# Two-layer hybrid decoder step on one core: in the prompt's attention, three PSUM banks for the turned probabilities and one for the results, in place of two and two

## The chip, the cores and the metric

One core of a Trainium2 chip runs the whole program. The metric is the device time of one execution in microseconds (us); of several runs the median counts. Engines are named as in the profile: PE (TensorE, matrix products; its weight loads are PEld), DVE (VectorE), ACT (ScalarE), POOL (GpSimd), SP (SyncE, which here only issues transfers). PSUM, into which PE writes, has 8 banks of 128 partitions by 512 fp32 values.

## The reference, cut to what matters

The program is one inference step of a two-layer decoder over 1024 prompt tokens and 32 new tokens. Layer 0 has sparse attention: an indexer has already chosen which keys each query may see, and the choice is an additive mask. The change concerns the prompt's attention alone:

```
s = einsum('nqgrd,nqkgd->nqgrk', q, k) * HEAD_DIM ** -0.5     # 8 heads, 2 key-value heads, HEAD_DIM 128
s = where(valid, s, -inf)
p = softmax(s, axis=-1)
o = einsum('nqgrk,nqkgd->nqgrd', p, v)                        # then o @ w_o, residual, MLP, layer 1, ...
```

## The kernel before

The program is a row of blocks, each with one stream of instructions for every engine, written by hand and tied by semaphores. Within a stream the order is as written: an instruction that waits holds back everything behind it on its engine. The block that changes is the prompt's attention, L1787 to L1917. The blocks before it leave the queries in `qt`, keys in `kt`, values in `vr`, the indexer's scores in `score`; the block after it multiplies the results, which lie in `qt`, by `w_o`.

The prompt's 1024 rows are 8 tiles of 128 rows (t = 0 to 7), and each tile has 8 heads, so `qk_list` has 64 entries, called steps n = 0 to 63 here, with t = n // 8. Step n needs keys of t + 1 tiles only. Each step runs through all engines:

- PE, `qk(n)`, L1809: products of queries and keys into one of two pairs of banks (banks 2 and 3, or 4 and 5). It waits until DVE has read the products of step n - 2.
- DVE, L1909 to L1912: adds the mask, takes the row's maximum, and negates it.
- ACT, L1865: the exponential, with the row's sum. DVE, L1883: the reciprocal of that sum (it stands in DVE's loop behind the maximum of the step after). POOL, L1876: the scaling.
- PE, `turn(n)`, L1820: turns the probabilities, tile by tile of 128 by 128, into a bank of their own, up to four tiles to a bank; so a step has one such filling for t up to 3 and two from t = 4 on. ACT, L1856: copies each filling into `pt`.
- PE, `pv(m, part)`, L1832: the products of probabilities and values. They are made for four heads at once (m = 0 to 15, two for each tile), in one bank, and a group's t + 1 products are spread over four parts, one to each iteration of PE's loop. DVE, `take_pv(m)`, L1888: copies the bank's 512 columns into `qt`.

PE's loop runs qk(n), turn(n - 3), then one part of `pv`: the part of n is `divmod(n - 7, 4)`. DVE's loop runs, for n: in tiles t = 2 to 6 from the second head on one of seven passes that make the next tile's mask (`mask_steps`, L1617 to L1633), then the maximum of step n, then the reciprocal of step n - 1, and in every fourth iteration one `take_pv`: `take_pv(m)` stands in iteration n = 11 + 4 m. In that same iteration PE's `pv(m + 1, 0)` stands, behind qk(n) and turn(n - 3). ACT's loop runs the exponential of n and then the copies of step n - 3.

The banks before: 0 and 1 by turns for results, 2 to 5 for the scores, 6 and 7 by turns for turned probabilities. The waits that go with them, in PE's stream:

```
if m >= 2: pe.wait_ge(p_copied, m - 1)     # turn: the filling two back has been copied by ACT
if m >= 2: pe.wait_ge(pv_empty, m - 1)     # pv, part 0: the result two back has been copied by DVE
```

For t = 0 to 2 part 0 of a group has no product (it holds products 0 to (t + 1) // 4 - 1), but its waits stand there all the same. Its other wait, for the copies of the group's last head, is in both kernels.

Of the kernel before, what the change touches and what calls it, by code (L numbers as in the profile page):

```python
# [24 lines left out]
GROUP = HEADS // KV  # L25
# [7 lines left out]
P = 128  # L33
# [110 lines left out]
def hybrid_step(nc, x_prompt, x_sample, cache_k, cache_v, cache_kidx, state_pool, page_table, c_prompt, c_sample,  # L144
# [3 lines left out]
    with ctx:  # L148
# [43 lines left out]
        vr = sb("vr", [P, TILES + 1, KW])  # L192
# [109 lines left out]
        pt = [put("pt0", [P, TILES, GROUP * P]), at("pt1", [P, TILES, GROUP * P], F32, whi.manual_sbuf_range[0])]  # L302
# [4 lines left out]
        def bank(i):  # L307
            return pair[i // 2][:, i % 2, :]
# [17 lines left out]
        def sem(name):  # L326
            return ctx.enter_context(nc.semaphore(name))
# [43 lines left out]
        p_t, p_copied, pv_ready, pv_empty = sem("p_t"), sem("p_copied"), sem("pv_ready"), sem("pv_empty")  # L371
# [111 lines left out]
        def raw8(slot):  # L483
            return wraw[:, slot, :].rearrange("p (k c) -> p k c", k=KT8)
# [1299 lines left out]

        qk_list = [(t, h) for t in range(TILES) for h in range(HEADS)]  # L1787
        turn_list = [(t, h, a) for t, h in qk_list for a in range((t + 4) // 4)]
        PV_AFTER = AHEAD + GROUP
        with nc.Block() as block:  # L1790
            @block.sync
            def _(sp):
                for u in range(U_O, U_O + 2):
                    load_unit(sp, u, raw8(u % 2), dsa_w_o[0, :, (u - U_O) * P:(u - U_O + 1) * P].rearrange(
                        "(k p) c -> p k c", p=P))

            def turns_of(n):
                return [(m, a) for m, (t, h, a) in enumerate(turn_list) if (t, h) == qk_list[n]]

            @block.tensor  # L1800
            def _(pe):
                def qk(n):
                    t, h = qk_list[n]
                    if n >= 2:
                        pe.wait_ge(neg_done, n - 1)
                    L = P * (t + 1)
                    for s in range((L + 511) // 512):
                        w = min(512, L - 512 * s)
                        ins = pe.matmul(pair[1 + n % 2][:, s, 0:w], qt[:, h, t * P:(t + 1) * P],  # L1809
                                        kt[:, h // GROUP, 512 * s:512 * s + w], start=True, stop=True)  # L1810
                    ins.then_inc(qk_ready, 1)

                def turn(n):
                    t, h = qk_list[n]
                    pe.wait_ge(prob_done, n + 1)
                    for m, a in turns_of(n):
                        if m >= 2:
                            pe.wait_ge(p_copied, m - 1)
                        for j in range(4 * a, min(4 * a + 4, t + 1)):
                            ins = pe.transpose(bank(6 + m % 2)[:, (j - 4 * a) * P:(j - 4 * a + 1) * P],  # L1820
                                               ss[:, n % SR, j * P:(j + 1) * P], ident)
                        ins.then_inc(p_t, 1)

                def pv(m, part):

                    t, g = divmod(m, KV)
                    if part == 0:
                        pe.wait_ge(p_copied, turns_of(GROUP * m + GROUP - 1)[-1][0] + 1)
                        if m >= 2:
                            pe.wait_ge(pv_empty, m - 1)  # L1830
                    for j in range(part * (t + 1) // GROUP, (part + 1) * (t + 1) // GROUP):
                        ins = pe.matmul(bank(m % 2), vr[:, j, g * P:(g + 1) * P], pt[m % 2][:, j, :], start=(j == 0),  # L1832
                                        stop=(j == t))
                    if part == GROUP - 1:
                        ins.then_inc(pv_ready, 1)

                N = len(qk_list)
                for n in range(N + PV_AFTER):
                    if n < N:
                        qk(n)  # L1840
                    if 0 <= n - AHEAD < N:
                        turn(n - AHEAD)
                    if n >= PV_AFTER:
                        pv(*divmod(n - PV_AFTER, GROUP))

            @block.scalar
            def _(act):
                def copies(n):
                    t, h = qk_list[n]
                    for m, a in turns_of(n):  # L1850
                        act.wait_ge(p_t, m + 1)
                        k = min(4, t + 1 - 4 * a)
                        q = 2 * t + h // GROUP
                        if h % GROUP == 0 and q >= 2:
                            act.wait_ge(pv_ready, q - 1)
                        act.activation(pt[q % 2][:, 4 * a:4 * a + k, (h % GROUP) * P:(h % GROUP + 1) * P],  # L1856
                                       bank(6 + m % 2)[:, 0:k * P].rearrange("p (j c) -> p j c", j=k),
                                       ACT.Copy).then_inc(p_copied, 1)

                N = len(qk_list)  # L1860
                for n in range(N + AHEAD):
                    if n < N:
                        L = P * (qk_list[n][0] + 1)
                        act.wait_ge(neg_done, n + 1)
                        act.activation(ss[:, n % SR, 0:L], ss[:, n % SR, 0:L], ACT.Exp,  # L1865
                                       bias=small[:, 4 + n % SR:5 + n % SR],
                                       scale=SC_ATT, accum_out=small[:, 8 + n % SR:9 + n % SR]).then_inc(exp_done, 1)
                    if n >= AHEAD:
                        copies(n - AHEAD)

            @block.gpsimd
            def _(pool):
                for n, (t, h) in enumerate(qk_list):
                    L = P * (t + 1)
                    pool.wait_ge(rec_done, n + 1)
                    pool.tensor_scalar(ss[:, n % SR, 0:L], ss[:, n % SR, 0:L], small[:, 12 + n % SR:13 + n % SR], None,  # L1876
                                       ALU.mult).then_inc(prob_done, 1)

            @block.vector
            def _(dve):  # L1880
                def recip(n):
                    dve.wait_ge(exp_done, n + 1)
                    dve.reciprocal(small[:, 12 + n % SR:13 + n % SR], small[:, 8 + n % SR:9 + n % SR]).then_inc(rec_done, 1)  # L1883

                def take_pv(m):
                    t, g = divmod(m, KV)
                    dve.wait_ge(pv_ready, m + 1)
                    dve.tensor_copy(qt[:, GROUP * g:GROUP * (g + 1), t * P:(t + 1) * P],  # L1888
                                    bank(m % 2).rearrange("p (r c) -> p r c", r=GROUP)).then_inc(pv_empty, 1)


                chain(dve, dve.memset(causal[:, 0:P], 0.0), "v", vchain)
                chain(dve, dve.tensor_copy(causal[:, P:2 * P], cst[:, C_CM:C_CM + P]), "v", vchain)
                N = len(qk_list)
                for n in range(N + PV_AFTER + 1):
                    if n < N:
                        t, h = qk_list[n]
                        L = P * (t + 1)
                        mask = score_of(t) if t in IDX_TILES else causal[:, P - t * P:2 * P]
                        if t + 1 in IDX_TILES[1:]:  # L1900

                            if h == 0:
                                masking = mask_steps(dve, COL_OF[t + 1])
                            else:
                                next(masking)
                        dve.wait_ge(qk_ready, n + 1)
                        if n >= SR:
                            dve.wait_ge(p_t, turns_of(n - SR)[-1][0] + 1)
                        chain(dve, dve.tensor_tensor_reduce(ss[:, n % SR, 0:L], wide(1 + n % 2)[:, 0:L], mask, 1.0,  # L1909
                                                            LEAST, ALU.add, ALU.max, small[:, n % SR:n % SR + 1]),  # L1910
                              "v", vchain)
                        dve.tensor_scalar(small[:, 4 + n % SR:5 + n % SR], small[:, n % SR:n % SR + 1], -SC_ATT, None,  # L1912
                                          ALU.mult).then_inc(neg_done, 1)
                    if 1 <= n <= N:
                        recip(n - 1)
                    if n >= PV_AFTER + GROUP and (n - PV_AFTER) % GROUP == 0:
                        take_pv((n - PV_AFTER) // GROUP - 1)  # L1917
# [623 lines left out]
```

## Time and profile before

| | |
|---|---|
| time, median of 3 runs | 2372.76 us (2372.74 to 2382.14) |
| the profiled execution | 2369.18 us, of which 2367.5 us are the span from first to last instruction |
| busy in the span | PE 2232.2 us (94%), DVE 1001.8 (42%), ACT 782.0 (33%), POOL 634.6 (27%) |
| the block of the change | from 489.7 us (first of L1809) to 661.6 us (last products of L1832) |

Times in the rows are us from the span's start. A row of the timeline has start, duration, engine, line, operation, output and inputs, shapes and count, and in brackets how long the engine stood idle before it and what released it. Ends of matmuls are modelled, and neighbours overlap by about 0.16 us in the rows: the 592 ns of a 128x512 product are spaced by 430 ns when PE runs on. An fp32 product shows as two records, a turned tile as one.

### The profile page before, as it was taken

How to read it: one execution, taken by the hardware profiler on the slowest of the kernel's cores; microseconds unless marked ns; L12 is line 12 of the kernel's file. 1: busy time of each engine (PE TensorE's matmuls, PEld its weight loads, DVE VectorE, ACT ScalarE, POOL GpSimd, SP SyncE). 2: the span in 40 equal slices, each digit the busy share in tenths (PEclk: the TensorE clock that was granted, in tenths of full speed). 3: DMA queues.
4: the chain of work that ended last, by engine and by line, in shares of the span. 5: the costliest groups of instructions: out<-in, count | busy, mean ns of one | idle time of the engine just before them, and what ended most of it. 6: DMA issues, size and time to landing. Idle time of an engine off the chain costs nothing. (4 is left out here: it accounts for less than half of the span.)

```text
span 2367.5 us, 37205 instructions
## 1 busy us (share of the span) xinstructions
PE 2232.2 (94%) x13836; PEld 2056.8 (87%) x13836; DVE 1001.8 (42%) x2431; ACT 782.0 (33%) x1414; POOL 634.6 (27%) x387
## 2 busy tenths in 40 slices
PE   5998899589989999999999999888999999999998
PEld 4885489245578999999999999888999999999998
DVE  2525788776435433233233332357333333323323
ACT  4204577655533312212212212354122122122124
POOL 4110111257736222222222222432222222222224
PEclk8998999889999999999999999899999999999999
DMA  8454464400032111111111112001111111111112
GB/s 301 140 171 128 148 207 156 144 18 1 0 127 80 54 45 50 49 44 44 44 44 51 46 44 65 27 19 45 46 45 45 44 46 52 45 44 44 44 44 82
DMA packets 208668, 170.29 MB, mean 72 GB/s; under 512 B 14477, under 2 KB 202109, under 8 KB 208565
## 3 DMA queue, kind: packets, MB, share of 16 engines
q1 hardware_dynamic: 201917, 154.64, 21.0%
q10 hardware_dynamic: 4160, 8.65, 1.0%
q0 software_dynamic: 2496, 5.77, 0.9%
q8 instruction: 55, 0.90, 0.2%
q14 instruction: 40, 0.33, 0.0%
HBM read 155.85 MB, written 11.64 MB: 71 GB/s over the span
## 5 line engine op out<-in xcount | busy, mean ns | idle before, releaser
L524 PE MATMUL pair<-hhi,whi 128*128 128x352 f32 x2184 | 716.6, 328 | 33.9 <-DVE hlo L725 8.8
L525 PE MATMUL pair<-hlo,whi 128*128 128x352 f32 x2184 | 705.0, 323 | 0.0
L526 PE MATMUL pair<-hhi,wlo 128*128 128x352 f32 x2184 | 704.6, 323 | 0.0
L2143 POOL TENSOR_TENSOR wlo<-wraw,whi 128x1024 fp32r<-128x1024 f32 x127 | 304.6, 2399 | 1145.1 <-ACT whi L2088 1143.9
L524 PE MATMUL pair<-hidh,whi 128*128 128x352 f32 x1536 | 495.4, 323 | 0.0
L525 PE MATMUL pair<-hidl,whi 128*128 128x352 f32 x1536 | 492.7, 321 | 0.0
L526 PE MATMUL pair<-hidh,wlo 128*128 128x352 f32 x1536 | 492.2, 320 | 0.0
L536 DVE SCALAR_TENSOR_TENSOR x<-pair,mod,x 128x352 f32<-128x352 f32 (+1 forms) x432 | 247.4, 573 | 514.6 <-PE pair L526 513.6
L524 PEld LDWEIGHTS pair<-hhi,whi 128*128 128x128 f32 x2184 | 412.3, 189 | 45.3 <-issue 25.0
L525 PEld LDWEIGHTS pair<-hlo,whi 128*128 128x128 f32 x2184 | 413.5, 189 | 0.4
L526 PEld LDWEIGHTS pair<-hhi,wlo 128*128 128x128 f32 x2184 | 412.3, 189 | 0.5
L2088 ACT ACTIVATE whi<-wraw 128x1024 fp32r<-128x1024 f32 x126 | 132.7, 1054 | 609.6 <-PE pair L526 609.6
L2195 DVE TENSOR_TENSOR squ<-relu 128x352 f32<-128x352 f32 x192 | 101.3, 527 | 492.0 <-ACT relu L2096 491.9
L525 PEld LDWEIGHTS pair<-hidl,whi 128*128 128x128 f32 x1536 | 288.5, 188 | 0.0
L524 PEld LDWEIGHTS pair<-hidh,whi 128*128 128x128 f32 x1536 | 288.3, 188 | 0.0
L526 PEld LDWEIGHTS pair<-hidh,wlo 128*128 128x128 f32 x1536 | 287.9, 187 | 0.0
L2096 ACT ACTIVATE relu<-pair 128x352 f32<-128x352 f32 x192 | 89.2, 464 | 471.1 <-PE pair L526 471.1
L494 POOL TENSOR_TENSOR wlo<-wraw,whi 128x1024 fp32r<-128x1024 f32 x36 | 89.1, 2476 | 282.0 <-ACT whi L490 281.9
L1876 POOL TENSOR_SCALAR ss<-ss,small 128x128 f32<-128x128 f32 (+7 forms) x64 | 118.5, 1856 | 79.9 <-DVE small L1883 79.5
L2199 DVE TENSOR_TENSOR hidl<-squ,hidh 128x352 fp32r<-128x352 f32 x192 | 105.0, 547 | 21.1 <-DVE squ L2195 1.9
L1452 ACT ACTIVATE junk_a<-score,cand 128x1024 f32<-128x1024 f32 (+2 forms) x93 | 84.0, 903 | 42.6 <-DVE cand L1533 31.2
L2098 ACT ACTIVATE hidh<-relu 128x352 fp32r<-128x352 f32 x192 | 95.9, 499 | 6.1
(282 smaller groups left out, 1955.3 us busy)
## 6 DMA issues: line engine op xcount, KB each, us to landing
wraw<-in_w_up_dram SPq DMA_DIRECT2D x64, 512.0 KB, 3.9
wraw<-in_w_down_dram SPq DMA_DIRECT2D x64, 512.0 KB, 3.4
mraw_i<-in_w_mod_dram SPq DMA_DIRECT2D x20, 1024.0 KB, 6.8
mraw_q<-in_w_mod_dram SPq DMA_DIRECT2D x12, 1024.0 KB, 5.1
mraw<-in_w_mod_dram SPq DMA_DIRECT2D x8, 1024.0 KB, 9.2
wraw<-in_dsa_w_in_dram SPq DMA_DIRECT2D x16, 512.0 KB, 6.0
mraw_w<-in_w_mod_dram SPq DMA_DIRECT2D x8, 1024.0 KB, 5.2
wraw<-in_dsa_w_o_dram SPq DMA_DIRECT2D x16, 512.0 KB, 4.1
```

The source lines that it names most:

```text
L494: pool.tensor_tensor(wlo[:, slot, :], wraw[:, slot, :], whi[:, slot, :], ALU.subtract).then_inc(lo_ready, 1)
L524: pe.matmul(out, a, hi[:, kr, r], start=(n == 0), stop=False)
L525: pe.matmul(out, a, lo[:, kr, r], start=False, stop=False)
L526: last = pe.matmul(out, b, hi[:, kr, r], start=False, stop=(n == len(ks) - 1))
L536: ins = dve.scalar_tensor_tensor(out=xs, in0=ps[:, 0:n], scalar=mod[:, layer, gate + d, 0:1], in1=xs, op0=ALU.mult, op1=ALU.add)
L1876: pool.tensor_scalar(ss[:, n % SR, 0:L], ss[:, n % SR, 0:L], small[:, 12 + n % SR:13 + n % SR], None, ALU.mult).then_inc(prob_done, 1)
L2088: act.activation(whi[:, slot(k), :], wraw[:, slot(k), :], ACT.Copy).then_inc(hi_ready, 1)
L2096: act.activation(relu[:, p % 3, :], up_bank(f, c, first)[:, 0:CW], ACT.Relu).then_inc(up_empty, 1)
L2098: act.activation(hidh[:, f, c * CW:(c + 1) * CW], relu[:, p % 3, :], ACT.Square).then_inc(square_done, 1)
L2143: pool.tensor_tensor(wlo[:, slot(k), :], wraw[:, slot(k), :], whi[:, slot(k), :], ALU.subtract).then_inc(lo_ready, 1)
L2195: dve.tensor_tensor(squ[:, p % 3, :], relu[:, p % 3, :], relu[:, p % 3, :], ALU.mult).then_inc(hid_square, 1)
L2199: dve.tensor_tensor(hidl[:, f, c * CW:(c + 1) * CW], squ[:, p % 3, :], hidh[:, f, c * CW:(c + 1) * CW], ALU.subtract).then_inc(hid_ready, 1)
```

## The change

The turned probabilities go through three banks by turns, 6, 7 and 1, and PE waits for the copy of the filling three back. All results go into bank 0, and part 0 of a group waits until DVE has copied the group just before. The copies of ACT and DVE read the banks so chosen. Nothing else differs.

```diff
+        T_BANK = (6, 7, 1)
 ...
                     for m, a in turns_of(n):
-                        if m >= 2:
-                            pe.wait_ge(p_copied, m - 1)
+                        if m >= 3:
+                            pe.wait_ge(p_copied, m - 2)
                         for j in range(4 * a, min(4 * a + 4, t + 1)):
-                            ins = pe.transpose(bank(6 + m % 2)[:, (j - 4 * a) * P:(j - 4 * a + 1) * P],
+                            ins = pe.transpose(bank(T_BANK[m % 3])[:, (j - 4 * a) * P:(j - 4 * a + 1) * P],
                                                ss[:, n % SR, j * P:(j + 1) * P], ident)
 ...
                     if part == 0:
                         pe.wait_ge(p_copied, turns_of(GROUP * m + GROUP - 1)[-1][0] + 1)
-                        if m >= 2:
-                            pe.wait_ge(pv_empty, m - 1)
+                        if m >= 1:
+                            pe.wait_ge(pv_empty, m)
                     for j in range(part * (t + 1) // GROUP, (part + 1) * (t + 1) // GROUP):
-                        ins = pe.matmul(bank(m % 2), vr[:, j, g * P:(g + 1) * P], pt[m % 2][:, j, :], start=(j == 0),
+                        ins = pe.matmul(bank(0), vr[:, j, g * P:(g + 1) * P], pt[m % 2][:, j, :], start=(j == 0),
                                         stop=(j == t))
 ...
                         act.activation(pt[q % 2][:, 4 * a:4 * a + k, (h % GROUP) * P:(h % GROUP + 1) * P],
-                                       bank(6 + m % 2)[:, 0:k * P].rearrange("p (j c) -> p j c", j=k),
+                                       bank(T_BANK[m % 3])[:, 0:k * P].rearrange("p (j c) -> p j c", j=k),
                                        ACT.Copy).then_inc(p_copied, 1)
 ...
                     dve.tensor_copy(qt[:, GROUP * g:GROUP * (g + 1), t * P:(t + 1) * P],
-                                    bank(m % 2).rearrange("p (r c) -> p r c", r=GROUP)).then_inc(pv_empty, 1)
+                                    bank(0).rearrange("p (r c) -> p r c", r=GROUP)).then_inc(pv_empty, 1)
```

## Rows read from the trace of the kernel before

**Rows 1.** Busy time by stretch (its us, busy by engine, granted clock, transfers).

```profile
core 0: us, PE busy (x) PEld busy (x) DVE busy (x) ACT busy (x) POOL busy (x), PEclk, DMA share, GB/s
489.00:497.00 8.00, 6.71 (x25) 5.19 (x26) 4.90 (x38) 4.63 (x21) 4.24 (x7) 0.57 0.48 134
497.00:520.00 23.00, 20.74 (x84) 11.59 (x83) 18.79 (x81) 14.66 (x48) 17.67 (x16) 1.00 0.00 1
...
583.00:612.00 29.00, 28.26 (x109) 15.45 (x108) 19.16 (x40) 15.15 (x32) 21.73 (x8) 1.00 0.00 1
612.00:645.00 33.00, 33.00 (x124) 17.68 (x123) 13.28 (x39) 17.31 (x33) 22.14 (x9) 1.00 0.00 0
...
662.00:670.00 8.00, 2.25 (x8) 2.28 (x9) 5.07 (x7) 6.26 (x14) 3.45 (x2) 0.62 0.78 286
```

**Rows 2.** Waits of PE in the block: who for whom, us, times, longest.

```profile
PE pair L1820 <- ACT pt L1856: 4.5, 10, 1.1
PE pair L1820 <- POOL ss L1876: 2.6, 5, 0.9
```

**Rows 3.** Timeline around iteration 59 (tile 7).

```profile
626.91 1.23 DVE L1909 CUSTOM_DVE_ANT_0 ss<-pair,score 128x1024 f32<-128x1024 f32 x1 [2.71 <-PE pair L1809]
627.59 1.02 PE L1832 MATMUL pair<-pt,vr 128*128 128x512 f32 x2
...
628.32 0.67 DVE L1888 COPY qt<-pair 128x512 f32<-128x512 f32 x1
```

**Rows 4.** Timeline: PE released by DVE in iteration 13.

```profile
500.71 0.15 DVE L1912 TENSOR_SCALAR small<-small 128x1 f32<-128x1 f32 x1
...
500.92 0.70 PE L1809 MATMUL pair<-kt,qt 128*128 128x256 f32 x2
```

**Rows 5.** Timeline around iteration 11 (tile 1).

```profile
500.26 0.60 PE L1809 MATMUL pair<-kt,qt 128*128 128x256 f32 x2
...
500.86 0.67 DVE L1888 COPY qt<-pair 128x512 f32<-128x512 f32 x1
```

**Rows 6.** Timeline around iterations 27 to 29 (tile 3).

```profile
525.46 1.11 PE L1809 MATMUL pair<-kt,qt 128*128 128x512 f32 x2
...
526.19 0.67 DVE L1888 COPY qt<-pair 128x512 f32<-128x512 f32 x1
...
526.84 1.56 DVE L1626 TENSOR_TENSOR_SCAN tie_run<-tie 128x640 f32<-128x640 f32 x1
...
528.43 0.69 DVE L1909 CUSTOM_DVE_ANT_0 ss<-pair,score 128x512 f32<-128x512 f32 x1
```

**Rows 7.** Timeline around iteration 31 (tile 3).

```profile
534.31 1.02 PE L1832 MATMUL pair<-pt,vr 128*128 128x512 f32 x2
...
535.04 0.67 DVE L1888 COPY qt<-pair 128x512 f32<-128x512 f32 x1
```

**Rows 8.** Timeline of iterations 43 to 45 (tile 5).

```profile
568.11 1.02 PE L1832 MATMUL pair<-pt,vr 128*128 128x512 f32 x2
...
568.89 0.67 DVE L1888 COPY qt<-pair 128x512 f32<-128x512 f32 x1
...
570.59 0.85 PE L1820 MATMUL pair<-cst,ss 128*128 128x128 f32 x6 [0.17 <-ACT pt L1856]
...
571.88 0.96 DVE L1909 CUSTOM_DVE_ANT_0 ss<-pair,score 128x768 f32<-128x768 f32 x1
...
574.72 0.84 PE L1820 MATMUL pair<-cst,ss 128*128 128x128 f32 x6 [1.13 <-ACT pt L1856]
```

**Rows 9.** Timeline of the block's end.

```profile
646.72 1.06 PE L1820 MATMUL pair<-cst,ss 128*128 128x128 f32 x8 [0.77 <-ACT pt L1856]
...
654.52 2.74 PE L1832 MATMUL pair<-pt,vr 128*128 128x512 f32 x6
654.72 0.69 DVE L1888 COPY qt<-pair 128x512 f32<-128x512 f32 x1 [8.44 <-PE pair L1832]
654.95 0.19 PEld L1832 LDWEIGHTS pair<-pt,vr 128*128 128x128 f32 x1 [0.24 <-issue]
```

## Prediction

> **What bounds the kernel now.** I first read the busy time by stretch. Over the block's last full tile, from 612 to 645 us, PE is busy for 33.00 of 33 us and nobody else for more than 22.14; in tile 6 it is 28.26 of 29; from tile 1 to the middle of tile 2 it is 20.74 of 23, with DVE at 18.79 [rows 1]. So PE sets the pace in the late tiles, and PE and DVE take turns in the early ones. The granted clock is 1.00, the level of 2.4 GHz, from 497 us on. The waits of PE come next: in the whole block it waited 4.5 us, in 10 places, for ACT's copies of turned probabilities, and 2.6 us for POOL [rows 2]. No row names a wait of PE for `pv_empty`: with two result banks that copy was always in time. Last I read the timeline at the places where the copy of a result and the next group's first products meet, iterations 11, 15, ... 67, fifteen in all.
>
> **What the change removes.** A third bank lets a filling start one copy earlier. All that it can give is what rows 2 show: 4.5 us. As the modelled ends overlap their successors by some 0.16 us, each of the 10 waits is really longer by that: 6.1 us at most, and nothing at least. Instructions, shapes and transfers stay as they were. The copies of ACT and DVE read other banks at the same price as long as nobody else touches those banks, and the semaphores see to that.
>
> **What it adds: a wait behind DVE's copy, fifteen times.** Take iteration 59. PE runs qk(59), turn(56), and then wants `pv(13, 0)`, whose first product starts at 627.59. With one bank it must wait for `take_pv(12)`. DVE issues that copy in the same iteration, behind the maximum of step 59 (1.23 us from 626.91), and this maximum had itself waited 2.71 us for qk(59). So the copy runs from 628.32 to 629.00 (0.67 us) [rows 3], 1.41 us after PE wants its bank. The copy is not slow; it is queued behind work that PE itself has only just released. Nothing makes DVE earlier when PE is later.
>
> To the difference comes the release. In iteration 13 PE started 0.06 us after DVE's negation had ended (500.86 to 500.92) [rows 4]. Then a weight load, 0.19 us [rows 9], must be made that normally lies under the product before. So 0.06 us if none of it shows, 0.25 if all; I take 0.15. One stall is then the copy's end, less the start that PE would have had, plus 0.15 us: 1.56 us in iteration 59.
>
> Behind the waiting part stand, on PE, the group's products, qk(n + 1) and turn(n - 2); DVE's next maximum waits for that qk, ACT's exponential for DVE, POOL for both. All move together, so a stall costs its whole length, unless PE would soon have waited for somebody who is not late.
>
> **The sum, in three parts.**
>
> *Iterations 11 to 27, five stalls* whose part 0 has no product; what waits is qk(n + 1). In the first, qk(12) starts at 500.26 and the copy ends at 501.53 [rows 5]; as PE next waited for POOL anyway, I count 0.8 us of it. In the last, qk(28) starts at 525.46 and the copy ends at 526.86 [rows 6]: about 1.5. The three between give about 1.1, 0.9 and 1.5 in the same reading, together some 5.8. In those of iterations 19 and 27 DVE goes straight from the copy into the scan of the mask pass (1.56 us from 526.84), and the next maximum, at 528.43, waits for the scan and not for qk(28), which even with the stall ends near 527.9. So I let most of these two, 1.6 us, be swallowed: **4.2 us** remain.
>
> *Iterations 31 to 55, seven stalls* with products. The first is 534.31 against a copy that ends at 535.71, 1.56 us with the release [rows 7]; that of iteration 43 is 568.11 against 569.56, 1.60 [rows 8]; the one of iteration 39, 1.5, is shorter in the rows only because PE had waited for ACT before it, and the other four lie between 1.5 and 1.65. Together 11.05 us. Here the third bank gives back. After iteration 43, PE waited 0.17 us and then 1.13 us for ACT's copies [rows 8], which came late because DVE's scan had pushed the maximum to 571.88. Now PE comes later by 1.6 us, DVE and ACT do not, and the first filling needs no fresh copy, so 1.6 us of it are gone again by iteration 45. In the same way I count back 1.45 in iterations 36 and 37, 0.35 each in 39 and 41, 0.2 in 50 and 0.85 in 52 and 53: 4.8 us in all, and **6.25 us** remain.
>
> *Iterations 59, 63 and 67.* Tile 7 has no mask pass, and PE does not wait. The stalls are 1.56, 1.55 and, in the drain, where the copy (654.72 to 655.41) no longer stands behind a maximum and the product would start at 654.52, 1.04 [rows 9]. Before turn(61) PE waited 0.77 us for ACT [rows 9], 0.93 without the overlap, and that is regained. **3.2 us** remain.
>
> The sum is 4.2 + 6.25 + 3.2 = 13.65 us: 21.0 us of stalls less 7.35 given back. The block's end moves by that, and with it the rest of the program: the next block's first work reads the last results, and its transfers are issued behind them. The profiled execution would go from 2369.18 to 2382.8 us, its span from 2367.5 to 2381.2. The median of the runs lies 3.6 us above the profiled execution; I put the same difference on it: 2372.76 + 13.65 = 2386.4 us, 0.58% slower.
>
> One rule of the Trainium skill speaks directly against the change. "Perfetto Trace Analysis", in the section on optimizing tensor performance, says that independent matmul groups should rotate through different PSUM banks, so that the evacuation of one overlaps the next group's matmuls. Priced as that sentence reads, one evacuation laid bare per group, it would be 15 times the copy's 0.67 us and the release, some 12 us before anything is given back. Rows 3 make it twice as dear, because the copy stands behind a maximum in DVE's queue.
>
> **The rivals.**
>
> *Nothing is given back.* If every wait for DVE, ACT and POOL moves along with PE, all 21.0 us stay: 2393.8 us. The rows of iterations 43 to 45 speak against it, since there DVE runs on its own work [rows 8]; for it speaks that in most iterations DVE had waited for qk. Chance 0.1.
>
> *The stalls of tiles 1 to 6 are swallowed* (the other side: not slower by what can be measured). Place: the mask pass of each tile, where DVE leads. If the two stalls of each tile, some 3.1 us, fit into the time by which PE is ahead of DVE and ACT there, only tile 7's 3.2 us remain: 2376.0 us. It decides from about 1.9 us given back by chance beyond my count, since 11.8 us is the bound below. For it: tile 5 swallows its first stall whole. Against it: in tile 6 PE stands idle for only 0.74 of 29 us [rows 1]. Chance of this and what lies between it and the bound: 0.22.
>
> *Only the gain.* If DVE's copy were in time, for a reason that I do not see in rows 3, the 6.1 us at most would be left: 2366.7 us, 0.26% faster and still no measurable change. Chance 0.03. The change can hardly be faster by more than 0.5%.
>
> *The clock falls.* The stalls thin PE's work most in tile 1. The granted clock was 0.57 and 0.62 in the stretches on both sides of the block, where PE stood still between products or for 6 us [rows 1]. If one stretch like that at the block's head, some 7 us, came back at 1.2 GHz, half of it, 3.4 us, would be added: 2389.8 us. Against it: it stayed at 1.00 through waits of up to 1.1 us [rows 1, 2]. Chance 0.07.
>
> **How the numbers follow.** What a measurement can tell from no change is 0.5%, 11.9 us, so the bound lies at 2384.6. My forecast holds with a chance of 0.58 and runs from 2381.5 to 2391 by itself: the release at 0.06 or 0.25 us over some eleven uncovered stalls makes 1 us either way, and what is given back, 4.5 by rows 2 alone or up to 9, makes 2 to 3. A sixth of it lies under the bound. Slower: 0.48 + 0.1 + 0.07, about 0.65; the same 0.33; faster 0.02. The range reaches toward the swallowed case and toward the one with nothing given back: 2377 to 2392.
>
> **What would show it.** In the profile after: about nine gaps of 1.2 to 1.6 us before the products or the weight loads of L1832, put down to the copy of L1888, and five more before L1809; PE's wait for ACT's copies well under 4.5 us; the maximum of step 59 with a longer idle time than 2.71 us only in the iteration after a stall; tile 7 longer by some 3 us. It would be wrong if the copies ended before PE wanted the bank, if iterations 44 and 45 kept their waits for ACT, or if the granted clock left 1.00 inside the block.

## The result, and the profile after

| | before | after |
|---|---|---|
| time, median of 18 runs each | 2373.76 us (2369.69 to 2382.14) | 2387.66 us (2380.61 to 2393.16) |
| ratio after to before | | 1.0056, 95% interval 1.0046 to 1.0065 |
| profiled span | 2367.5 us | 2389.4 us |
| attention block, from the first score product to the end of the last result copy | 489.70 to 662.28: 172.6 us | 497.11 to 683.20: 186.1 us |

The kernel became 0.56% slower, 13.3 us of 2373.76 by the ratio (10.9 to 15.4 by the interval); forecast were 13.65 us and 0.58%. The two profiled spans lie 21.9 us apart, and that is not the price: 13.5 us of it lie in the block, 7.4 us ahead of it and 1.0 behind it, where nothing was changed. In the ten profiles of this study the block begins anywhere from 489.7 to 497.1 us, so the kernels are compared by the block's length below, each taken from one profile, beside the timed runs.

PE's waits from 490 us on, through the block and just past it (who for whom: us, times, longest):

```profile
PE pair L1833 <- DVE qt L1889: 13.7, 10, 1.5
...
PE pair L1810 <- issue: 5.1, 4, 1.3
PE pair L1810 <- ACT pt L1857: 1.4, 1, 1.4
...
PE pair L1821 <- POOL ss L1877: 0.8, 3, 0.4
```

Line numbers after are one higher than before. The first three rows are the fifteen new stalls. Ten stand before the products of L1833 and are named rightly. Five stand before qk, where part 0 of the group has no product, and are put down to other things: "issue", or ACT's copy. The timelines tell what they wait for: each of the five starts some 0.1 us after the result's copy has ended. Here is qk(28):

```profile
537.34 0.67 DVE L1889 COPY qt<-pair 128x512 f32<-128x512 f32 x1
...
537.99 1.55 DVE L1626 TENSOR_TENSOR_SCAN tie_run<-tie 128x640 f32<-128x640 f32 x1
...
538.12 1.10 PE L1810 MATMUL pair<-kt,qt 128*128 128x512 f32 x2 [1.34 <-issue]
...
539.58 0.69 DVE L1910 CUSTOM_DVE_ANT_0 ss<-pair,score 128x512 f32<-128x512 f32 x1
```

Together the three rows are 20.2 us. Of the third, 0.4 us stood at the same place, before qk(20), in the kernel before:

```profile
PE pair L1809 <- ACT pt L1856: 0.4, 1, 0.4
```

On the other side PE's 4.5 us behind ACT's copies [rows 2] have no row left before the turns, and its 2.6 us behind POOL have become 0.8. The balance is 20.2 - 0.4 - 4.5 - 1.8 = 13.5 us, and the block grew by 13.5.

Iteration 59 after, to be laid beside [rows 3]:

```profile
644.53 1.22 DVE L1910 CUSTOM_DVE_ANT_0 ss<-pair,score 128x1024 f32<-128x1024 f32 x1 [2.71 <-PE pair L1810]
...
645.94 0.67 DVE L1889 COPY qt<-pair 128x512 f32<-128x512 f32 x1
...
646.75 1.10 PE L1833 MATMUL pair<-pt,vr 128*128 128x512 f32 x2 [1.39 <-DVE qt L1889]
```

DVE's rows are those of before, shifted. PE starts its products 2.22 us after the maximum has begun, where before it was 0.68: 1.54 us later. The first two products take 1.10 us in place of 1.02: part of the weight load is laid bare, which starts 0.03 us ahead of them here and 0.11 ahead before. The stall costs 1.62 us; 1.56 were forecast.

Iterations 43 to 45, beside [rows 8]:

```profile
583.80 1.10 PE L1833 MATMUL pair<-pt,vr 128*128 128x512 f32 x2 [1.44 <-DVE qt L1889]
...
586.02 0.82 PE L1821 MATMUL pair<-cst,ss 128*128 128x128 f32 x6
586.32 0.96 DVE L1910 CUSTOM_DVE_ANT_0 ss<-pair,score 128x768 f32<-128x768 f32 x1 [0.39 <-DVE tie_run L1626]
...
588.83 0.82 PE L1821 MATMUL pair<-cst,ss 128*128 128x128 f32 x6
```

From the products of iteration 43 to the turn of iteration 45 it is 5.03 us here, and 6.61 before: once PE has stalled, it no longer waits for ACT, and 1.58 us are given back.

### The profile page after: what moved, and what is told of

It is laid out like the page before. It is cut to its first block and busy times, and to the rows that moved or that the text cites. A ratio compares the mean times of both kernels' runs of the same rounds, so it can differ in the third digit from the quotient of the medians.

```text
span 2389.4 us, 37204 instructions
## 1 busy us (share of the span) xinstructions
PE 2238.2 (94%) x13836; PEld 2060.9 (86%) x13836; DVE 1002.2 (42%) x2431; ACT 781.6 (33%) x1414; POOL 636.0 (27%) x387
```

## The experiments

Block lengths are from the profiles, ratios from the timed runs against the kernel before. One thing in the lengths is not the edits': up to qk(11), which comes before the first stall, the block takes 9.4 us in two of the runs (one result bank with two turned banks; changed without mask passes) and 9.9 to 10.0 in the other eight. The granted clock over the block's first 9 us is 0.81 in those two and 0.62 in the others. Where it matters, the length counted from qk(11) is given too.

| run | block, us | ratio, 95% interval |
|---|---|---|
| before | 172.6 | |
| changed | 186.1 | 1.0056 (1.0046 to 1.0065) |
| one result bank, two turned banks | 187.6 | 1.0066 (1.0049 to 1.0082) |
| changed, copy before the maximum | 167.9 | 0.9961 (0.9947 to 0.9975) |
| before, copy before the maximum | 169.6 | 0.9986 (0.9974 to 0.9997) |
| one result bank, two turned banks, copy before the maximum | 171.3 | 0.9987 (0.9974 to 1.0001) |
| before, no mask passes | 166.7 | 0.9978 (0.9965 to 0.9991) |
| changed, no mask passes | 184.2 | 1.0055 (1.0034 to 1.0076) |
| changed, copy before the maximum, last group apart | 166.8 | 0.9972 (0.9960 to 0.9983) |
| changed, copy one step later | 198.4 | 1.0135 (1.0111 to 1.0160) |

**Half of the change: one result bank, two turned banks.** The turns and ACT's copies keep to banks 6 and 7, and the turns wait for the copy two back.

```diff
-        T_BANK = (6, 7, 1)
+        T_BANK = (6, 7)
 ...
-                        if m >= 3:
-                            pe.wait_ge(p_copied, m - 2)
+                        if m >= 2:
+                            pe.wait_ge(p_copied, m - 1)
 ...
```

> One result bank as in the change, but two banks for the turned probabilities as before. Lengths are of the attention block, from its first score product to the end of its last result copy: 172.6 us before, 186.1 after. Theory (what is given back comes from ACT and DVE not being late while PE is): the block is within 1.5 us of that after, 185 to 187.6, since after a stall the copies are long done; PE's waits for ACT's copies add up to under 2 us. Rival (the third bank gives it back): the 4.5 to 6.1 us of waits for copies return, block 190 to 192.

Measured: 187.6 us, 1.5 more than the changed kernel, or 2.0 counted from qk(11). PE's waits in that profile:

```profile
PE pair L1833 <- DVE qt L1889: 13.2, 10, 1.5
...
PE pair L1821 <- ACT pt L1857: 1.2, 6, 0.3
```

The waits for ACT before the turns fall from 4.5 to 1.2 us without any third bank. What was given back is for the most part not the third bank's; its share beside the stalls is about 2 us.

**The copy ahead of the maximum.** In DVE's loop `take_pv` is moved from the end of its iteration to just before the wait for the score products.

```diff
+                    if n >= PV_AFTER + GROUP and (n - PV_AFTER) % GROUP == 0:
+                        take_pv((n - PV_AFTER) // GROUP - 1)
+                    if n < N:
                         dve.wait_ge(qk_ready, n + 1)
 ...
                     if 1 <= n <= N:
                         recip(n - 1)
-                    if n >= PV_AFTER + GROUP and (n - PV_AFTER) % GROUP == 0:
-                        take_pv((n - PV_AFTER) // GROUP - 1)
```

> The changed kernel, with DVE's copy of a result put ahead of the maximum of its iteration (behind the mask pass's step) instead of behind it. Theory (the stall is the queue in front of the copy, not the copy): the copy then runs under the score products and the turns, the stalls before the products go, only the one in the drain stays, and the third bank's gain shows: block 167 to 173 us, kernel between 6 us faster and no different from before. Rival (one bank bares the copy itself, 0.67 us and the release of 0.15, fifteen times): 12 us of stalls less some given back, block 178 to 184.

Measured: 167.9 us, 18.2 less than the changed kernel and 4.7 less than before. Iteration 59 of that run:

```profile
623.68 1.88 PE L1810 MATMUL pair<-kt,qt 128*128 128x512 f32 x4
623.88 0.69 DVE L1889 COPY qt<-pair 128x512 f32<-128x512 f32 x1 [0.99 <-PE pair L1833]
...
625.39 1.04 PE L1821 MATMUL pair<-cst,ss 128*128 128x128 f32 x8
625.60 1.23 DVE L1913 CUSTOM_DVE_ANT_0 ss<-pair,score 128x1024 f32<-128x1024 f32 x1 [1.02 <-PE pair L1810]
626.27 1.02 PE L1833 MATMUL pair<-pt,vr 128*128 128x512 f32 x2
```

The copy lies wholly under the score products, in time in which DVE had been idle, and the products start 0.67 us after the maximum, as before the change. The same bank, the same copy, one place earlier in a queue: the stall is gone. Of the waits for a result's copy that of the drain is left, 0.9 us, and in the first tiles four before qk: three of 0.1 to 0.2 us, and one of 0.6 before qk(20), which the profile puts down to ACT's copy though qk(20) starts 0.1 us after the result's copy has ended. With two result banks and the same move, below, PE waits 0.5 us at that place.

By the timed runs this kernel is 9.3 us faster than the one before (5.9 to 12.6), more than the 6 expected at most and more than the block's 4.7. No run shows where the rest lies.

**The same move in the kernel before.**

> The kernel before, with the same move of DVE's copy. Theory: with two result banks the copy was in time anyway, so block 171.6 to 174 us, no measurable change. Rival (the move itself helps or harms, since the maximum and with it ACT and POOL come 0.7 us later in every fourth iteration): off by more than 2 us.

Measured: 169.6 us, 3.0 less than before, so the theory as written fails here, and the rival holds. The copy did cost the kernel before something. DVE's timeline of iterations 43 and 44:

```profile
568.03 0.69 DVE L1888 COPY qt<-pair 128x512 f32<-128x512 f32 x1 [0.59 <-PE pair L1832]
569.25 0.96 DVE L1912 CUSTOM_DVE_ANT_0 ss<-pair,score 128x768 f32<-128x768 f32 x1 [0.53 <-PE pair L1809]
...
570.45 2.01 DVE L1626 TENSOR_TENSOR_SCAN tie_run<-tie 128x896 f32<-128x896 f32 x1
572.49 0.96 DVE L1912 CUSTOM_DVE_ANT_0 ss<-pair,score 128x768 f32<-128x768 f32 x1
```

From maximum to maximum it is 3.24 us. In the kernel before the copy stood between the first maximum and the scan [rows 8], and it was 4.13 (567.75 to 571.88):

```profile
567.75 0.96 DVE L1909 CUSTOM_DVE_ANT_0 ss<-pair,score 128x768 f32<-128x768 f32 x1 [1.90 <-issue]
...
569.54 2.30 DVE L1626 TENSOR_TENSOR_SCAN tie_run<-tie 128x896 f32<-128x896 f32 x1
```

Of the 0.89 us between them 0.67 is the copy; the scan is 0.29 longer there, for a reason that was not looked for. ACT's loop makes the exponential of a step ahead of the copies of the step three back, so a late maximum makes these copies late, and PE's turns wait for them: 4.5 us before, 1.9 here, and POOL's 2.6 became 1.7.

**One result bank, two turned banks, and the move.** This has both edits shown above.

> One result bank, two turned banks, DVE's copy ahead of the maximum. Beside the run with three turned banks and the same move it prices the third bank where no stall hides it. Theory (the waits of PE for ACT's copies come back as in the kernel before): 2 to 5 us longer than that run, block 171 to 176 us. Rival (a third bank gives nothing, as the turn waits for POOL or DVE anyway): within 1 us of it.

Measured: 171.3 us, 3.4 more than with the third bank. PE waits 1.9 us for ACT's copies before the turns, against 0.2 with the third bank. Against the run with two result banks and the same move (169.6) the single result bank costs 1.7 us, 0.9 of it the drain's stall. With the copy behind the maximum the same step, from two result banks to one, cost 15.0 us (187.6 against 172.6). Two turned banks stand in all four of these kernels: the price is set by the copy's place in DVE's queue.

**No mask passes.** The seven steps of a pass are replaced by one memset, in the kernel before and in the changed one. These two kernels leave out the choice of keys in tiles 3 to 7.

```diff
-                            if h == 0:
-                                masking = mask_steps(dve, COL_OF[t + 1])
-                            else:
-                                next(masking)
+                            if h == 1:
+                                chain(dve, dve.memset(score_of(t + 1), 0.0), "v", vchain)
```

> The kernel before without the mask passes of tiles 3 to 7: in place of seven steps for each tile, one memset of the scores, so that these tiles attend to every key of their rows. Theory (PE's waits for ACT in tiles 2 to 6 come from these steps on DVE): PE's wait for ACT's copies falls from 4.6 us to under 1.5, block 166 to 169 us against 172.6. Rival (two turned banks are short by themselves): the waits stay, block 171 to 173.

> The changed kernel without the mask passes, as in the run beside it. Theory (stalls are given back only where DVE and ACT lead by the mask passes): the stalls now cost 18 to 21 us in place of 13.5 against the run beside it, block 185 to 189 us. Rival (what is given back is the third bank's): the difference between the two stays at 13 to 15 us, block 180 to 183.

Measured: 166.7 and 184.2 us, a difference of 17.5 where the kernels with mask passes differ by 13.5. The first run is as its theory had it, with 1.5 us of waits for ACT left. In the second the difference and the block fall a little short of the 18 and the 185 forecast. Its first steps were 0.6 us shorter, as said above: counted from qk(11) the two differ by 18.1 us, against 13.5 with the passes. So 4.6 us of what is given back is theirs.

**The copy one step later.** In DVE's loop of the changed kernel `take_pv` is moved behind the next iteration's mask step.

```diff
+                    if n > PV_AFTER + GROUP and (n - 1 - PV_AFTER) % GROUP == 0:
+                        take_pv((n - 1 - PV_AFTER) // GROUP - 1)
+                    if n < N:
                         dve.wait_ge(qk_ready, n + 1)
 ...
                     if 1 <= n <= N:
                         recip(n - 1)
-                    if n >= PV_AFTER + GROUP and (n - PV_AFTER) % GROUP == 0:
-                        take_pv((n - PV_AFTER) // GROUP - 1)
```

> The changed kernel with DVE's copy of a result moved further back by one item of DVE's queue, behind the next iteration's mask step (in every second group of tiles 2 to 6 that is the scan, five of them, 9.7 us together in the kernel before). Theory (a stall is as long as the queue in front of the copy): the five stalls grow by the scans, block 186.1 plus 8 to 11 us, 194 to 197. Rival (the number of banks sets the price, not DVE's order): 186 to 188.

Measured: 198.4 us, 12.3 more than the changed kernel, in the direction of the theory and 1.4 us above its range. (By the timed runs it is 32 us slower than the kernel before, 26.3 to 38.0, where the block has 25.8; no run shows the difference.) The scans:

```profile
L1626 DVE TENSOR_TENSOR_SCAN tie_run<-tie 128x512 f32<-128x512 f32 (+4 forms) x5 | 8.7, 1748 | 0.0
```

8.7 of the 12.3 us are the scans themselves; PE's waits for the copy grew by 9.1, from 20.2 to 29.3. The rest is PE's clock. Its timeline at iteration 35, and the granted clock (third number from the end) in stretches around it and around iteration 51:

```profile
556.12 0.71 PE L1821 MATMUL pair<-cst,ss 128*128 128x128 f32 x5
560.09 2.05 PE L1833 MATMUL pair<-pt,vr 128*128 128x512 f32 x2 [3.27 <-DVE qt L1889]
561.93 1.93 PE L1810 MATMUL pair<-kt,qt 128*128 128x512 f32 x4
```

```profile
555.00:562.00 7.00, 3.73 (x13) 1.98 (x12) 4.05 (x10) 2.97 (x7) 5.41 (x2) 0.85 0.00 0
562.00:569.00 7.00, 7.00 (x31) 4.22 (x30) 3.92 (x11) 3.04 (x8) 3.91 (x2) 0.91 0.00 0
...
620.00:630.00 10.00, 9.44 (x30) 5.10 (x31) 3.95 (x8) 2.00 (x4) 5.49 (x2) 0.83 0.00 0
```

After the gap of 3.27 us two products take 2.05 us in place of 1.02: PE runs at 1.2 GHz. At half speed, a mean of 0.85 over 7 us means 2.1 us spent there; with 1.3 in the next stretch and 3.4 around iteration 51 that is 6.8 us, of which half, 3.4, is lost by this estimate. 8.7 + 3.4 = 12.1.

**The version that the runs point to: the last group apart.** The changed kernel with the copy ahead of the maximum, and the results of the last group in bank 2, which the scores have left by then.

```diff
+        def pv_bank(m):
+            return bank(2 if m == LAST else 0)
 ...
-                        if m >= 1:
+                        if m == LAST:
+                            pe.wait_ge(neg_done, len(qk_list) - 1)
+                        elif m >= 1:
                             pe.wait_ge(pv_empty, m)
 ...
-                        ins = pe.matmul(bank(0), vr[:, j, g * P:(g + 1) * P], pt[m % 2][:, j, :], start=(j == 0),
+                        ins = pe.matmul(pv_bank(m), vr[:, j, g * P:(g + 1) * P], pt[m % 2][:, j, :], start=(j == 0),
 ...
```

> The changed kernel with DVE's copy ahead of the maximum, and the last group's result in bank 2, which the scores no longer need, so that no stall is left in the drain. Theory: 1.0 us shorter than the run with the copy ahead of the maximum, block 166.9 us (166.4 to 167.4), no wait of PE for a result's copy of more than 0.1 us. Rival (the drain's stall is hidden by something else): block 167.9.

Measured: 166.8 us, 1.1 less than with the move alone. The drain's stall is gone; the waits before qk in the first tiles stay as they were, so that PE still waits more than the 0.1 us expected for a result's copy. The last groups' products run in one piece:

```profile
654.81 7.46 PE L1840 MATMUL pair<-pt,vr 128*128 128x512 f32 x17
```

Both versions beat the kernel before in the timed runs, by 0.39% and 0.28%. Their intervals overlap, so that 1.1 us is shown by the block alone.

## Why the prediction was right

By its three parts, from the timelines of both kernels, each counted from its block's first product:

| up to | grown by, forecast | measured |
|---|---|---|
| qk of iteration 31 (533.01 before, 544.66 after) | 4.2 | 4.24 |
| qk of iteration 56 (612.33 before, 630.01 after) | 10.45 | 10.27 |
| the block's end | 13.65 | 13.5 |

- *Where the stalls come from.* Right, and shown from both sides. With the copy one place earlier in DVE's queue all but the drain's go, or shrink to a small rest in the first tiles; one place further back the five with a scan in front of the copy grow by that scan. The signs that were named came too: ten waits before the products, nine of 1.39 to 1.46 us and the drain's of 0.88, and five before qk of 1.20 to 1.36.
- *Their sum.* 21.0 us forecast. The wait rows have 20.2, but they lack the modelled overlap and the longer products. From the starts of PE's instructions, laid beside those of the kernel before, the fifteen stalls come to 22.7. Of the 1.7 more, 0.6 is the first stall, which the forecast counted without what PE would have waited for POOL; the rest is mostly the release. It took 0.10 to 0.15 us, and the bared weight load another 0.07 before the products, where 0.15 was taken for both.
- *What is given back.* 7.35 us forecast; about 6.3 in the wait rows, and 22.7 - 13.5 = 9.2 by the starts of PE's instructions. Both terms were too small by nearly the same amount, so that the net came within 0.15 us is in part luck. The prediction gave two reasons at once, that ACT and DVE are not late and that a third bank needs no fresh copy, and did not part them. The runs do: without the third bank all but about 2 us stays given back. By itself, where no stall hides it, the bank is worth 3.4 us, inside its bounds of nothing and 6.1. 4.6 us hang on the mask passes, as argued. The two shares may overlap, and what remains was not followed.
- *The rivals.* "Nothing is given back" and "the stalls of tiles 1 to 6 are swallowed" are both refuted by the table: from iteration 31 to 56 the block grew by 6.0 us, and not by the 11 of the stalls or by nothing. "The clock falls" did not happen: the granted clock stayed at 1.00 from 505 us to the end of the block, with gaps of up to 1.5 us. It can happen here nonetheless, since it set in when the gaps were made longer.
- *What the prediction had wrong without harm.* It said that with two result banks the copy was always in time. PE never waited for it, but through the scan and ACT it cost the kernel before 3.0 us. The forecast compares against that kernel, so its sum does not contain this.

The Trainium skill's sentence in "Perfetto Trace Analysis", in the section on optimizing tensor performance, that independent groups should rotate through PSUM banks, is borne out in direction: 1.0066 with one result bank and the turned banks left as they were. What the runs add is that here rotation mattered mostly because of the queue in front of the evacuation: a single bank costs 15.0 us of block with the copy behind the maximum and 1.7 with it ahead, the latter in the drain and in the first tiles.

## What to carry to other kernels

Here a buffer taken away cost what stood in front of its release in the releasing engine's queue, far more than the release itself takes. So look at which instruction of that queue is waiting for the engine that you are about to stall. Before giving a stage another bank, try to move the small copy into a place where its engine is idle; here one moved statement was worth 18 us of the changed kernel and 3 us of the one before. And a stall's price is not its length: subtract the waits that it makes needless, and check that the gap leaves the clock alone.

## What was not expected of the hardware

PE's clock did not follow the length of a gap alone. In the run with the copy one step later the products behind a gap of 3.27 us ran at 1.2 GHz at once (two of them in 2.05 us). After one of 3.85 us the granted clock fell about 0.8 us after PE had begun again: the group's two products took 1.30 us, and the four records of the next qk 3.19, where those of the step before had taken 1.67. After one of 3.56 us, in iteration 43, the clock stayed at 2.4 GHz:

```profile
588.82 1.10 PE L1833 MATMUL pair<-pt,vr 128*128 128x512 f32 x2 [3.56 <-DVE qt L1889]
...
620.56 1.30 PE L1833 MATMUL pair<-pt,vr 128*128 128x512 f32 x2 [3.85 <-DVE qt L1889]
621.66 3.19 PE L1810 MATMUL pair<-kt,qt 128*128 128x512 f32 x4
```

What decides between them was not tried. The head of the block shows the same kind of spread: over its first 9 us the granted clock was 0.62 in eight profiles and 0.81 in two, for the same work.
